# A decoder layer with 32 routed experts: overflow tiles run right behind their own expert on weights that are still in SBUF, experts change places by a table made on the chip, and the overflow tables are spread over ten gate steps

## What is computed

```python
grp = argmax(hf @ w_grp + b_grp)                    # one of 4 groups
in_grp = exp_logits[rows, grp]                      # its 8 experts
top_val, top_idx = top_k(in_grp, 2)
w_top = softmax(top_val) * grp_prob[grp]
for e in range(32):                                 # reference: dense
    a, u = hf @ w_e_gate[e], hf @ w_e_up[e]         # 1024 -> 256
    out += (silu(a) * u * gate[:, e:e + 1]) @ w_e_down[e]
```

## Time and profile before

| | us |
|---|---|
| runs (three) | 1174.81, 1174.98, 1181.34; median 1174.98 |
| the profiled execution | 1177.34 |
| its span, first to last instruction | 1175.6 |
| first gate and up product of the expert stage | starts at 809.76 |
| last scatter landed | 1151.1 |
| final norm and stores | to 1175.6 |

### The profile page before, as it was taken

One profiled execution on the slowest core, in us unless ns is written; L12 is line 12 of the kernel. 1 busy time (PEld: TensorE's weight loads), 2 busy tenths in 40 slices (PEclk: granted clock), 3 DMA queues, 4 the chain that ended last, 5 costly groups with the idle time before them and its releaser, 6 DMA issues.

```text
span 1175.6 us, 30447 instructions
## 1 busy us (share of the span) xinstructions
PE 1076.1 (92%) x12370; PEld 914.2 (78%) x12370; DVE 679.5 (58%) x1724; ACT 448.3 (38%) x761; POOL 255.9 (22%) x476
## 2 busy tenths in 40 slices
PE   6999899999999999999999899986999999999990
PEld 5989788778788888888877677775878887878870
DVE  5340435324666666666677533468767676766664
ACT  6321111221455555554577422221234333333323
POOL 1030000000333333221276300001232332322220
PEclk9999899999999999999999999996999999999995
DMA  9020855353656755565332355438999999999948
GB/s 366 18 90 3 291 179 161 108 164 141 156 119 165 214 126 119 134 139 127 104 80 57 133 214 179 135 143 298 329 366 369 359 357 357 342 363 363 361 110 299
DMA packets 62025, 239.19 MB, mean 203 GB/s; under 512 B 23328, under 2 KB 24128, under 8 KB 52032
## 3 DMA queue, kind: packets, MB, share of 16 engines
q1 hardware_dynamic: 54272, 220.45, 56.3%
q0 software_dynamic: 7616, 16.80, 6.2%
HBM read 201.14 MB, written 45.88 MB: 210 GB/s over the span
## 4 chain that ended last, share of the span: by engine, by line
PE 80%; DVE 6%; DMA 5%; issue 4%; ACT 2%; POOL 1%; SPq 1%; POOLq 0%; DVEq 0%; ACTq 0%
PE PS L2258 16%; PE PS L1920 13%; PE PS L2098 9%; PE PS L2268 8%; PE PS L2182 8%; PE PS L1909 6%; PE PS L2076 4%; PE PS L2037 4%; PE PS L2077 3%; PE PS L2249 3%; DMA wst<-in_wt 1%; DMA k<-T_d 1%; PE PS L1955 1%; PE PS L2070 1%; DVE wtl L1295 1%
## 5 line engine op out<-in xcount | busy, mean ns | idle before, releaser
L2258 PEld LDWEIGHTS PS<-XT,wgu 128*64 128x64 f32 x4352 | 186.9, 140 | 30.6 <-issue 29.2
L2258 PE MATMUL PS<-XT,wgu 128*64 128x96 f32 x4352 | 195.0, 251 | 16.1 <-issue 14.9
L1129 ACT ACTIVATE pt<-PS,cst 128x512 f32<-128x512 f32 (+3 forms) x288 | 167.2, 650 | 107.0 <-PE PS L2077 83.6
L1448 DVE CUSTOM_DVE_ANT_0 junkm<-PS,cst 128x512 f32<-128x512 f32 (+3 forms) x276 | 133.5, 532 | 76.6 <-PE PS L2037 74.5
L2098 PEld LDWEIGHTS PS<-V,pt 128*64 128x64 f32 x3840 | 121.2, 137 | 23.0 <-issue 11.5
L2098 PE MATMUL PS<-V,pt 128*64 128x65 f32 x3840 | 136.8, 225 | 0.9 <-issue 0.9
L1920 PE MATMUL PS<-hTh,wth 128*128 128x512 f32 x256 | 103.0, 403 | 4.6 <-DVE wtl L1295 4.6
L1920 PE MATMUL PS<-hTh,wtl 128*128 128x512 f32 x256 | 100.7, 393 | 0.0
L1920 PE MATMUL PS<-hTl,wth 128*128 128x512 f32 x256 | 100.7, 393 | 0.0
L843 POOL TENSOR_SCALAR_AFFINE_SELECT pt<-pt 128x128 f32<-128x128 f32 x224 | 64.0, 292 | 161.1 <-ACT pt L1129 118.4
L928 POOL DMA_INDIRECT x_d<-YO,ids x34 | 62.3, 1832 | 134.1 <-DVE YO L1811 104.6
(11 more groups left out here) (288 smaller groups left out, 1868.7 us busy)
## 6 DMA issues: line engine op xcount, KB each, us to landing
wgu<-in_wgu SPq DMA_DIRECT2D x34, 2048.0 KB, 16.6
wdn<-in_wdn SPq DMA_DIRECT2D x34, 1024.0 KB, 20.9
q<-T_d SPq DMA_DIRECT2D x58, 256.0 KB, 4.3
k<-T_d SPq DMA_DIRECT2D x58, 256.0 KB, 5.4
wst<-in_wt SPq DMA_DIRECT2D x16, 512.0 KB, 6.9
T_d<-thi SPq DMA_DIRECT2D x16, 512.0 KB, 2.6
T_d<-tlo SPq DMA_DIRECT2D x16, 512.0 KB, 3.9
xt<-in_x SPq DMA_DIRECT2D x8, 512.0 KB, 10.9
```

The source lines that it names most:

```text
L1129: ins = nc.scalar.activation(pt[:, (n + 2) % 6, 0:nt * P], PS[:, n % 3, 0:nt * P], ACT.Exp, scale=C("slopes", h, h + 1), bias=C("kb", w, w ...
L1448: V_.tensor_tensor_reduce(out=junk_[:, 0:L], in0=PS[:, bank, 0:L], in1=tab, scale=1.0, scalar=-3e38, op0=ALU.add, op1=ALU.max, accum_out=m ...
L2258: ins = mm(PS[h * HD:(h + 1) * HD, 2 + p, f * CAP:(f + 1) * CAP], wgu[q][:, c, lo:lo + HD], XT[:, p, c, :], start=(c == 0 and f == 0), sto ...
```

## The change

1. An overflow tile is put right behind a host, the expert whose overflow it is, and uses the host's weights from the same buffer. The places 15 and 23 of ORDER are the two hosts' (HOST, LABEL). A table `place_e` made on the chip lets an overfull expert of the places 8 to 31 swap places with the expert that stands there (`choose_hosts`); the lists and weights are swapped with it (`swap_ids`, `swap_weights`). So there are 32 loads instead of 34, and 32 splits of down weights. From place 8 on the SP engine reads the expert's number from the table.
2. An overflow tile and its neighbour can now share tokens wherever a swap has put an expert, so every scatter waits for the one before it.
3. The tables of the overflow tiles are spread over the gate steps 1 to 10 on VectorE; the 16 matmuls for their ids move from behind the first tile to behind the transposes in tile 9. `wdl` of tile 1 is made in gate step 0 as before, `wdl` of tile 0 now too.
4. Both halves of the output (but for the last tile) are copied by ScalarE.
5. The memory of the tables is needed longer, so the first 13 loads share five buffers; the sixth comes in with load 13, which waits for `wrow_ov` of gate step 10.
6. The last h2_d store is issued between the two parts of the load of tile 2, not behind both. In the first gate step the XT copy of tile 1 comes first.
7. Without an overflow that fits a host, such a tile runs in the loop behind the stage.

The diff, cut to its core:

```diff
+EARLY = 8
+HOST = (16, 24)
+TILE = (*ORDER[:HOST[0]], NE, *ORDER[HOST[0]:HOST[1]], NE + 1, *ORDER[HOST[1]:])
+LABEL = [ORDER[h - 1] for h in HOST]
+LOAD = [n - sum(n >= h + k for k, h in enumerate(HOST)) for n in range(NB)]
+DONE = [NB - 1 - LOAD[::-1].index(l) for l in range(NE)]
+SLOT = [l % 5 if l < 13 else (5, 3, 4, 0, 1, 2)[(l - 13) % 6] for l in range(NE)]
...
                 if t + 1 == NT:
                     sp_.wait_ge(g_mm, 2 * NT)
-                    load_expert(TILE[2], 2)
+                    sp_.dma_start(wgu[2][:], a["wgu"][TILE[2]].rearrange("p (k n) -> p k n", k=KC)).then_inc(we_in[2], 16)
                 h2_store(t, p)
+            sp_.dma_start(wdn[2][:], a["wdn"][TILE[2]].rearrange("p (k n) -> p k n", k=2)).then_inc(we_in[2], 16)
...
-            sp_.wait_ge(dve_did, DV.of("wrow_ov"))
-            load_expert(TILE[5], 5)
-            for n in range(RING, NB):
...
-                sp_.wait_ge(m_dn, n - RING + 1)
-                load_expert(e, n % RING)
+            for l in range(5, NE):
+                if PREV[l] is None:
+                    sp_.wait_ge(dve_did, DV.of("wrow_ov"))
+                else:
+                    sp_.wait_ge(m_dn, DONE[PREV[l]] + 1)
+                e = ORDER[l]
+                if l >= EARLY:
...
+                    e = sp_.value_load(place_e[0:1, e:e + 1], min_val=0, max_val=NE - 1)
+                load_expert(e, SLOT[l])
...
-                if TILE[n] >= NE or TILE[n - 1] >= NE:
+                if n >= 1:
                     pool.wait_ge(y_st[1 - p], 16 * ((n + 1) // 2))
...
                 copy(YO[0:CAP, p, 0:512], PS[0:CAP, 5, :], scale=wrow[0:CAP, col:col + 1]).then_inc(m_y0, 1)
+                if n < NB - 1:
+                    copy(YO[0:CAP, p, 512:D], PS[0:CAP, 6, :], scale=wrow[0:CAP, col:col + 1]).then_inc(m_y1, 1)
...
             m_x(0)
-            overflow_tables()
-            m_split_lo(0)
...
+            choose_hosts()
+            first_weights()
+            count_rest()
             for n in range(NB):
                 m_gate(n)
                 if n == 0:
-                    overflow_ids()
-                if n:
-                    m_out(n - 1)
-                if n + 1 < NB:
-                    m_split_lo(n + 1)
+                    m_split_lo(0)
+                if n + 1 < NB and LOAD[n + 1] != LOAD[n]:
+                    m_split_lo(LOAD[n + 1])
+                if n == 1:
+                    swap_ids()
+                if n == 2:
+                    swap_weights()
+                if n == 3:
+                    overflow_places()
+                if n == 4:
+                    places()
+                if n == 5:
+                    tiles_rows()
+                if n in (6, 7):
+                    tile_columns(n - 6)
+                if n == 8:
+                    overflow_rows()
+                if n == 9:
+                    overflow_experts()
+                if n == 10:
+                    overflow_ids()
...
             for n in range(NB):
                 m_up(n)
-                if n == 0:
-                    overflow_ids()
                 if n + 1 < NB:
                     m_transposes(n + 1)
+                if n == 9:
+                    overflow_ids()
```

252 lines of the change are left out of this document (163 added, 89 removed), and 4 rows, old and new, of the table DV.

## The result

The changed kernel takes 1187.03 us (median of seven runs, 1185.45 to 1194.03), beside 1176.91 for the kernel before on the same chip. The ratio is 1.0081, 95% interval 1.0053 to 1.0109: slower by 9.5 us, between 6 and 13. The profiled execution took 1185.64, of which 1183.9 are the span.

A forecast was written before the change was run, and what follows sets the result against it. TensorE was taken as the bound, at 9.65 us a tile, with the DMA engines at their limit beside it. Terms -2.5 - 2.8 + 1.5 - 1.6 + 6.0 + 17 = +17.6 gave 1192.5 us; own range 1186 to 1198, wider range 1166 to 1208.

The forecast's parts named there:

- likeliest class: Whole kernel: slower than before by over 1%, chance 0.60; within 1% had 0.29, faster by over 1% 0.11.
- (e): Overflow tables on VectorE in gate steps 1 to 10 make gates and XT copies late: +6.0 us, bounds 0 and 13.
- (f): Every scatter waits for the one before, step 11.3 to 11.8 against 9.65 a tile, biting from tile 17: +17, bounds 0 and +30.
- (a): Expert stage: two loads and two splits fewer, 6 MB; TensorE waits for no load, so 0.
- (b): Start of the stage: last h2_d store before tile 2's down weights, first gather earlier: -2.5 us, bounds 0 and -2.8.
- (c): Gap between first two products shrinks from 4.45 to 1.7: -2.8 us; the 16 id matmuls return in tile 9: +1.5.
- (d): Second product keeps the full clock after a shorter idle, 5.43 instead of 7.00: -1.6 us, bounds 0 and -1.6.
- (g): Five buffers up to load 12: load 5 some 8 us later, load 15 just in time: 0, bounds 0 and +4.
- R1: Rival: the chain of scatters doesn't bite, only start and tables count: +0.6 to +8, 1175.6 up to 1183; chance 0.28.
- R2: Rival: lighter DMA traffic takes away most stops inside TensorE's products and tables hide: -14, 1161; chance 0.11.
- R3: Rival: the DMA queue never empties, so the chain costs to the end: +0.6 + 30, 1206; chance 0.08.
- R4: Rival: an overflow tile finds no host and runs in the loop behind the stage, some 30 us each; chance 0.03.

The follow-up runs named there:

- late-load runs: Kernel before with load 5 held back until the first down product, alone (1.0044), or with the start's new order, where the moved overflow-expert table delayed load 5 (1.0054).
- the store alone: Kernel before with only the last h2_d store moved ahead of the down load of tile 2: 1.0010 of before.
- before, start: Kernel before with the store moved, first XT copy up into the tables, tile 1's transposes ahead of the id matmuls, its XT copy first in its gate: 0.9985.
- small pieces: Changed kernel, all waits kept, expert weights loaded in pieces of 4 KB per partition instead of 16 and 8 KB: 1.0017 of before.
- few waits: Changed kernel with scatters waiting for the one before only at tiles 16, 17, 21, 25 and 26: 0.9960 of before.
- light loads: Changed kernel, all waits kept, only half the gate/up weights loaded from load 5 on, so the output differs: 0.9882 of before.
- the gap alone: Kernel before with tile 1's transposes ahead of the id matmuls, its XT copy first in its gate, first wdl pair behind: 0.9979 of before.
- the late load: Kernel before with one edit, load 5 also waiting for the first down product: 1.0044 of before.

## Why the prediction was right, and where it was not

The forecast was 1192.5 with 1186 to 1198 as its own range; 1187.03 lies in it, and that is in part luck: the forecast stands on the median of 1174.98, the seven runs of before have 1176.91, and 1174.98 + 9.5 = 1184.5 would lie under the range. Its sum was +17.6 and the effect is +9.5, within 1% and not slower by over 1%, so its likeliest class was missed by a little. The mechanism, the chain of scatters, was right; the misses are in the size of terms, (e) by 5.3 and (f) by 2.8 above all.

(a) Two loads fewer, 0. Not tested alone. TensorE had no wait for weights before, which was my reason, and it is a poor one: in the late-load runs a hole that no product noticed came out as 4.6 and 6.0 us of such waits over a hundred us later. At 354 GB/s the 6.3 MB are some 18 us of the engines' time. They must be set against (g).

(b) The store, -2.5. The gather came earlier as said, but the store alone gave nothing; it needs the XT copy ahead of the tables, which the sum did not name. The first product is 3.7 earlier in the changed kernel; the two edits together gave 2.6 of it in "before, start", and the rest was not taken apart.

(c) The gap, -2.8 and +1.5. -2.4 in the kernel that has it alone. The gap is 1.51 in the changed kernel (804.37 + 6.77 to 812.65), I said 1.7. The 16 id matmuls made tile 9 1.4 longer (890.32 to 900.71, against 9.03).

(d) The clock, -1.6. Seen (7.00 to 5.50), and worth nothing: tile 1 to tile 2 is 10.5 in both kernels. VectorE makes two pairs of wdl in a row there, from 815.49 to 820.11, so gate step 1 starts late, its XT copy with it, and the third product waits for the copy. The gate step and the copy on VectorE, then the product, in the changed kernel:

```profile
820.03 0.35 DVE L1888 TENSOR_SCALAR ge<-PS 128x192 f32<-128x192 f32 x1
...
822.49 0.56 DVE L1875 COPY XT<-PS 128x384 f32<-128x384 f32 x1
```

```profile
823.15 5.50 PE L2375 MATMUL PS<-XT,wgu 128*64 128x96 f32 x128 [1.39 <-issue]
```

That is the 1.4 that (e) had for gate 1. The two cancel, and below they are both left out.

(e) The tables, +6.0. The most wrong in its sum, and nearly right gate by gate. The gate steps 1 to 9 start 1.9, 1.3, 0.4, 2.4, 0.9, 0.8, 0.1, 0.3 and 1.1 behind the end of their product, where I had 2.0, 1.6, 0.5, 2.7, 0.3, 1.4, 0, 0.5 and 1.3. From tile 1 to 9 the changed kernel's tiles take 5.5 more than 9.03 each, where I had 5.3. (My working does not give these figures from what it states: with 0.7 free a tile, 0.6 left over and 3.4 of tables make the second lateness 3.3 and not 1.6, and the whole cost some 15. An allowance that I did not write down is in them.) What failed is the comparison: the kernel before doesn't run at 9.03 there, it takes 4.1 more from tile 2 to 10 itself. From tile 2 to 10 the kernels without tables take 75.1 to 76.5, those with them 77.4 to 78.8 (the changed kernel in small pieces, at 81.0, left aside): +2.1, of which 1.4 are the id matmuls. So +0.7 or so. The late gates are there, as is the waiting for XT (4.0 us from 812 to 901, of which I had said about 6), but stops of before are not: its products of tiles 4 and 5 took 6.55 and 7.66 us, those of the changed kernel 5.59 and 5.50; one idle time stands in for the other. The bound "0 (the stops cover it)" was nearly it. Doubled, the same tables cost 13.5. That the missing stops are the cover is read from these traces; no run tests it by itself.

(f) The chain of scatters, +17. Measured 14.2, by taking it out. Right: the step (11.3 to 11.8 said, 11.65 in the mean), the catching up at tiles 9 to 11, the new start there. Off: it bites at tile 20 and not 17, and goes on at 11.8 a tile up to tile 27. The queue does run partly empty, as I said:

```profile
1060.00:1100.00 40.00, 34.10 (x505) 28.32 (x500) 20.55 (x34) 13.90 (x22) 12.15 (x8) 0.96 0.90 309
```

But the scatters stay 10.0 apart and more until a landing falls to 4.9 us at 1117.93, behind the last load (issued at 1100.23). The fixed cost plus bytes of the Trainium skill ("DMA: Bandwidth & Descriptors", section "Anatomy of one DMA — SWDGE (gpsimd) path"), by which there would be no loss at all, does not hold for a scatter beside the weights: 10.4 and a median of 10.6 from 920 to 1080 us, against its estimate of 2.9.

(g) Five buffers, 0, bound +4. TensorE waited 2.7 for the down weights of tiles 13 and 14. Behind that is a pause: the changed kernel moves 172 GB/s from 900 to 920 us, before 372.

```profile
900.00:920.00 20.00, 19.33 (x302) 16.19 (x302) 15.25 (x30) 7.90 (x13) 5.04 (x5) 1.00 0.62 172
```

That is 4.0 MB unmoved, and a hole at load 5 of about the same size cost 5.2 us. Whether (a) and (g) cancel in the changed kernel, or by how much, was not tried: the two terms were not taken apart. The kernel with few waits has both and is 4.7 faster than before, so together they cost it nothing that shows.

The sum anew: -3.7 - 2.4 + 1.4 + 0.7 + 14.2 = +10.2, against +9.5 measured. Without the chain it is -4.0, against -4.7. This agreement is closer than the terms allow: the first four are read from single traces at the start of the stage, only the last is a difference of timed runs, and the start's new order, which is -6.1 in this sum, gave a gain of 1.8 (at most 4.1) when it was timed by itself on the kernel before. The terms (a) and (g) are left out of it.

Of the rivals, R1 asked whether the chain bites; it does. R2 was faster by weaker stops: those inside products did fall, by 10, but in the changed kernel other waits stand in their place; its price shows in light loads. R3 (the queue never empties, +30) and R4 did not come.

Of the kernels that load all their weights, what beats both is the changed one with few waits, by 0.4% (interval 0.1 to 0.7), for this routing alone. The start's new order on the kernel before, which holds for any routing, gives 0.2% (the gap alone).

## What to carry to other kernels

Before a chain of waits is added to stores or scatters that add in place, compare one landing under load, not idle, with the pace of the loop: here it cost little where a landing was short (4.5 us in the pause) and up to the whole difference where the step was above the pace, and it also took away the catching up that hides other delays. Where the DMA engines' share is at its top for the rest of a stage, an idle hole in the loads can be a loss even if nothing needs a load there: load 5 issued 9 us later cost 5.2, as waits for weights that came 234 us behind it. And an instruction moved to the front gives nothing as long as the engine behind it has a queue, as the store alone showed; moving the pair brought the product forward by 2.6 and still gave no more in the timed runs than the gap alone. A line of waits called "issue" is worth taking apart by the timeline: here it hid waits for a copy.

## What the runs showed of the hardware

The time from issue to landing of the same 96-row scatter went from 4.33 to 11.6 with the weights in flight, and smaller pieces of the other queue's transfers shortened it by 1.3 at the median over the whole stage (9.7 to 8.4), at 309 and 312 GB/s.

TensorE's stops inside a product, with no releaser shown, are by its timelines 12.7 us in before, 13.2 with the late load, 8.8 with few waits, 2.5 in the changed kernel and 2.1 with light loads. One queue carries instructions there, in the changed kernel from 805 to 1150 us:

```profile
q8 instruction: 40, 0.66, 0.8%
```

These are packets of 16 KB, one in about 8.6 us. The Trainium skill ("Runtime: NRT & Kernel Launch", section "Instruction fetch mechanics") says that engines fetch their instructions in blocks of 16 KiB by a queue of their own, and that this is mostly hidden. The size agrees. That late blocks are the cause of the stops is a guess that no run here tests; what speaks for it is that they shrink when the other bytes do (8.8 to 2.1), and what speaks against it that smaller pieces changed nothing and that the changed kernel has only 2.5 of them with as many of these packets and its DMA engines as full.
